# State and offset products of a state-space mixer: fp32 against three fp32r passes in all blocks

## The reference

```python
cb = jnp.einsum('bclgn,bcsgn->bclsg', cc, bc)
y_diag = jnp.einsum('bclsgr,bcsgrp->bclgrp', cb[..., None] * decay, xdt)
decay_to_end = jnp.exp(a_cs[:, :, -1:] - a_cs)
states = jnp.einsum('bclgn,bclgr,bclgrp->bcgrpn', bc, decay_to_end, xdt)
chunk_decay = jnp.exp(a_cs[:, :, -1])
def step(carry, inp):
    st, dec = inp
    return carry * dec[..., None, None] + st, carry
...
y_off = jnp.einsum('bclgn,bcgrpn,bclgr->bclgrp', cc, prev, jnp.exp(a_cs))
```

## Time and profile before

| | us |
|---|---|
| median of 3 runs (lowest, highest) | 2748.22 (2746.03, 2751.57) |
| the profiled execution | 2746.11 |
| its span | 2744.4 |
| PE busy in it | 2702.8 (98%) |
| DVE, ACT, POOL busy | 1587.0, 1228.9, 1098.6 |
| mean granted clock of TensorE | 0.997 |

### The profile page before, as it was taken

The page is one execution under the profiler, slowest core; times in us unless marked ns, Lnnn a source line. Parts: engine busy times, 40 slices in busy tenths (PEclk is TensorE's granted clock), DMA queues, the critical chain, the costliest instruction groups (busy, mean ns, idle before and its releaser), DMA issues.

```text
span 2744.4 us, 37004 instructions
## 1 busy us (share of the span) xinstructions
PE 2702.8 (98%) x13938; PEld 2231.2 (81%) x13938; DVE 1587.0 (58%) x2093; ACT 1228.9 (45%) x2322; POOL 1098.6 (40%) x798
## 2 busy tenths in 40 slices
PE   8999999999999999999999999999999999999998
PEld 6778777888888888888888888888888888888887
DVE  3588742666425665147663466664445666666666
ACT  2366754455424555145542654555445322222323
POOL 1256642133201232003234587765555535353434
PEclk9999999999999999999999999999999999999999
DMA  9687576644556445565436546674434842333323
GB/s 290 200 270 243 202 253 245 264 146 181 201 199 254 179 146 206 193 231 217 167 144 250 187 160 221 240 275 155 164 133 171 345 153 94 142 117 135 118 92 154
DMA packets 225488, 531.10 MB, mean 194 GB/s; under 512 B 14090, under 2 KB 98062, under 8 KB 215838
## 3 DMA queue, kind: packets, MB, share of 16 engines
q1 hardware_dynamic: 225310, 528.74, 53.8%
HBM read 382.74 MB, written 145.95 MB: 193 GB/s over the span
## 4 chain that ended last, share of the span: by engine, by line
PE 92%; ACT 2%; DVE 2%; DMA 1%; issue 1%; SPq 1%; POOL 0%; DVEq 0%; ACTq 0%; POOLq 0%
PE bank L2047 22%; PE bank L2015 22%; PE bank L1725 19%; PE bank L1769 13%; PE bank L1749 6%; PE bank L1840 2%; PE bank L1847 2%; PE bank L1666 1%; PE bank L1821 1%; PE bank L1828 1%; PE bank L1804 1%; ACT E L1418 1%; PE bank L1788 1%; DMA meta_w<-in_w_in 0%; DMA w_scr<-w_both 0%
## 5 line engine op out<-in xcount | busy, mean ns | idle before, releaser
L1725 PE MATMUL bank<-hnT_hi,w_ring 128*128 128x512 f32 x1152 | 374.2, 396 | 0.2 <-DMA w_ring<-w_scr 0.2
L2166 DVE SCALAR_TENSOR_TENSOR acc<-pre,par,acc 128x512 f32<-128x512 f32 x240 | 216.3, 901 | 110.6 <-ACT pre L1276 104.9
L2047 PE MATMUL bank<-w_first,T_hi 128*128 128x512 f32 x896 | 275.9, 389 | 0.0
L1725 PEld LDWEIGHTS bank<-hnT_hi,w_ring 128*128 128x128 f32 x1152 | 216.4, 188 | 45.2 <-ACT win_tmp L1373 0.5
L2015 PE MATMUL bank<-T_hi,w_both 128*128 128x512 f32 x768 | 242.1, 389 | 0.2 <-DVE ff L2427 0.2
L2486 DVE TENSOR_TENSOR acc_th<-bank,acc_th 128x512 f32<-128x512 f32 x224 | 150.0, 686 | 155.3 <-PE bank L2047 155.1
L1769 PE MATMUL bank<-w_ring,T_hi 128*128 128x512 f32 x768 | 239.4, 393 | 0.0
L1029 POOL TENSOR_TENSOR small<-small 128x1 f32<-128x1 f32 (+1 forms) x71 | 17.1, 241 | 534.0 <-ACT yo L1356 334.6
L1725 PE MATMUL bank<-hnT_lo,w_ring 128*128 128x512 f32 x576 | 224.6, 390 | 0.0
L1749 PE MATMUL bank<-w_ring,hnT_hi 128*128 128x384 f32 x768 | 198.2, 339 | 0.0
L527 POOL TENSOR_TENSOR w_both<-raw,w_both 128x1024 fp32r<-128x1024 f32 x52 | 129.4, 2489 | 169.7 <-ACT w_both L519 169.6
(11 more groups left out here) (294 smaller groups left out, 6208.1 us busy)
## 6 DMA issues: line engine op xcount, KB each, us to landing
w_ring<-w_scr SPq DMA_DIRECT2D x312, 512.0 KB, 4.2
T_scr<-stage SPq DMA_DIRECT2D x32, 1792.0 KB, 6.6
w_scr<-w_both SPq DMA_DIRECT2D x104, 512.0 KB, 4.2
pair_raw<-in_w_ff SPq DMA_DIRECT2D x36, 1024.0 KB, 5.4
third<-T_scr SPq DMA_DIRECT2D x28, 1024.0 KB, 4.8
pair_raw<-T_scr SPq DMA_DIRECT2D x28, 1024.0 KB, 4.8
sums<-sums_scr SPq DMA_DIRECT2D x64, 384.0 KB, 4.9
raw<-in_w_in SPq DMA_DIRECT2D x36, 512.0 KB, 6.8
```

Of the source, the lines that this page charges most:

```text
L1725: mm = nc.tensor.matmul(bank[s][:, :], w[:, k, :], t[:, k, :], start=(k == 0 and j == 0), stop=(k == KT - 1 and j == 2))
L2047: mm = nc.tensor.matmul(bank[4 * half + t][:, :], a[:, k, tok], w[:, k, :], start=(SECOND[q % 7] not in GOES_ON and k == 0 and j == 0), st ...
L2166: ins = nc.vector.scalar_tensor_tensor(acc[:, s, 0:TB], pre[:, s, k:k + TB], w, acc[:, s, 0:TB], ALU.mult, ALU.add)
```

## The change

- `y_offset` and the state product become three fp32r passes each, in all four blocks. Their operands get high and low parts in new tiles laid over h: `c_both`, `s_both`, `xw_both`, and two of `b_both` in turn.
- Who makes them, in every step: ACT the high parts of C (128x128), S (128x384) and xw (128x384), and B's high part as a copy of its own (xb shrinks from 512 to 384 columns); POOL the low parts of C and S, ahead of its other mixer work; DVE the low part of B (from PSUM) and of xw.
- PE's step becomes: unit n1, `y_transposes` of q-2, `diagonal` of q-1, `slot1`, `state` of q-1, units n2, `y_offset`. So the fp32 work of a step stands in one stretch. `y_high` and `y_low` move one step later, ahead of xw's parts.
- On ACT the Exp now stands behind the high part of S, which waits for `state_add` of q-1; the high part of xw stands ahead of the block-0 weight splitting and the evacuation of n2. On DVE `state_add` moves ahead of the taps. On POOL S times decay moves ahead of ty += yo.
- The pooling history copies move from DVE to ACT, into the evacuation.
- The load of h moves from item 12 to unit (0, 4) of the out stage, behind the last state product.

```diff
-    def link(self, ins):
+    def mark(self, ins):
         self.n += 1
         ins.then_inc(self.sem, 1)
-        self.eng.wait_ge(self.sem, self.n)
+        return self.n
...
+        s_both = at("s_both", [P, 2, GW], h_at, F32R)
+        xw_both = at("xw_both", [P, 2, GW], h_at + 3072, F32R)
+        c_both = at("c_both", [P, 2, P], h_at + 6144, F32R)
+        b_both = [at(f"b_both{i}", [P, 2, P], h_at + 7168 + 1024 * i, F32R) for i in range(2)]
...
-                        if n == 12:
-
-                            sp.dma_start(h[:, :, :], x_in[0, b * TB:(b + 1) * TB, :].rearrange(
-                                "(t p) d -> p t d", p=P)).then_inc(h_loaded.sem, 16)
...
+                            if (d, i) == (0, 4):
+                                yoff_ps.wait(sp, b, STEPS)
+                                state_ps.wait(sp, b, STEPS)
+                                sp.dma_start(h[:, :, :], x_in[0, b * TB:(b + 1) * TB, :].rearrange(
+                                    "(t p) d -> p t d", p=P)).then_inc(h_loaded.sem, 16)
...
+                        cs_split_hi.wait(pool, b, 2 * q + 1)
+                        nc.gpsimd.tensor_tensor(c_both[:, 1, :], group_tile(g, 1)[:, c * P:(c + 1) * P],
+                                                c_both[:, 0, :].bitcast(F32), ALU.subtract)
+                        cs_split_hi.wait(pool, b, 2 * q + 2)
+                        nc.gpsimd.tensor_tensor(s_both[:, 1, :], S[:, g, :],
+                                                s_both[:, 0, :].bitcast(F32), ALU.subtract
+                                                ).then_inc(s_split_lo.sem, 1)
...
+                        gains_ready.wait(pool, b, 1)
+                        s_split_lo.wait(pool, b, q + 1)
+                        nc.gpsimd.tensor_tensor(by_head(S[:, g, :]), by_head(S[:, g, :]),
+                                                per_head(cd, c, g), ALU.mult
+                                                ).then_inc(scd_ready.sem, 1)
                         if b == 0:
                             low_part(pool, N0 + n2[0] + 2)
                         yo_ready.wait(pool, b, q + 1)
...
+                        yoff_ps.wait(act, b, q)
+                        nc.scalar.activation(c_both[:, 0, :], group_tile(g, 1)[:, c * P:(c + 1) * P],
+                                             ACT.Copy).then_inc(cs_split_hi.sem, 1)
                         sums_loaded[c].wait(act, b, 16 * (g + 1))
...
-                        fall.then_inc(fall_ready.sem, 1)
-                        fall_ready.wait(act, b, q + 1)
+                        falls = steps.mark(fall)
+                        state_ready.wait(act, b, q)
+                        nc.scalar.activation(s_both[:, 0, :], S[:, g, :], ACT.Copy
+                                             ).then_inc(cs_split_hi.sem, 1)
+                        steps.wait(falls)
                         nc.scalar.activation(E[:, :, :], E[:, :, :], ACT.Exp, scale=-1.0
                                              ).then_inc(exp_ready.sem, 1)
 
                         xb_ps.wait(act, b, q + 1)
-                        state_ps.wait(act, b, q)
                         ty_ready.wait(act, b, q)
                         xw_ready.wait(act, b, q)
-                        nc.scalar.activation(xb[:, :], bank[4 + q % 2][:, :], ACT.Copy
+                        nc.scalar.activation(b_both[q % 2][:, 0, :], bank[4 + q % 2][:, GW:GW + P],
+                                             ACT.Copy)
+                        nc.scalar.activation(xb[:, :], bank[4 + q % 2][:, 0:GW], ACT.Copy
                                              ).then_inc(xb_ready.sem, 1)
...
                         if q:
                             y_norm(b, q - 1)
+                        xw_ready.wait(act, b, q + 1)
+                        nc.scalar.activation(xw_both[:, 0, :], xw[:, :], ACT.Copy
+                                             ).then_inc(xw_split_hi.sem, 1)
                         if b == 0:
                             high_part(act, N0 + n2[0] + 2)
...
+                def y_offset(b, q):
+                    s_split_lo.wait(pe, b, q + 1)
+                    for j, (i, o) in enumerate(((0, 0), (0, 1), (1, 0))):
+                        mm = nc.tensor.matmul(bank[7][:, 0:GW], c_both[:, i, :], s_both[:, o, :],
+                                              start=(j == 0), stop=(j == 2))
+                    mm.then_inc(yoff_ps.sem, 1)
...
+                def state(b, q):
+
+                    xw_split_lo.wait(pe, b, q + 1)
                     yo_ready.wait(pe, b, q + 1)
...
                         if n1 is not None:
                             unit(b, n1)
+                        if q > 1:
+                            y_transposes(b, q - 2)
                         if q:
-                            slot3(b, q - 1)
+                            diagonal(b, q - 1)
                         slot1(b, q, g, c)
+                        if q:
+                            state(b, q - 1)
                         for n in n2:
                             unit(b, n)
-                        y_offset(b, q, g, c)
-                        if q:
-                            y_transposes(b, q - 1)
-                    slot3(b, STEPS - 1)
+                        y_offset(b, q)
+                    y_transposes(b, STEPS - 2)
+                    diagonal(b, STEPS - 1)
+                    state(b, STEPS - 1)
...
                         if q:
                             y_finish(b, q - 1)
+                            state_add(b, q - 1)
                         taps(b, n1)
-                        if q:
-                            state_add(b, q - 1)
...
+                        nc.vector.tensor_tensor(b_both[q % 2][:, 1, :], bank[4 + q % 2][:, GW:GW + P],
+                                                b_both[q % 2][:, 0, :].bitcast(F32), ALU.subtract)
...
+                        if q > 1:
+                            y_low(b, q - 2)
+                        xw_low(b, q)
```

More of the change, by code:

```diff
@@ L1246, in _ @@
                 high_part(act, 1)
+                steps = Steps(act, act_sem)
                 def evac(b, v):
@@ L1269, in evac @@
                         w3 = par[:, W_CONV + 60 + ct:W_CONV + 61 + ct]
-                        nc.scalar.activation(pre[:, s, 0:3], hist[:, ct, :], ACT.Copy
-                                             ).then_inc(hist_read.sem, 1)
+                        hist_read = steps.mark(nc.scalar.activation(
+                            pre[:, s, 0:3], hist[:, ct, :], ACT.Copy))
                         nc.scalar.activation(acc[:, s, 0:TB], ps, ACT.Identity, scale=w3,
                                              bias=par[:, W_BIAS + ct:W_BIAS + ct + 1])
-                        hist_read.wait(act, b, sum(conv_tile(m) is not None for m in range(n + 1)))
+                        steps.wait(hist_read)
                         nc.scalar.activation(hist[:, ct, :], ps[:, TB - 3:TB], ACT.Copy)
@@ L1282, in evac @@
                     else:
-                        nc.scalar.activation(pre[:, s, 16:16 + TB], ps, ACT.Copy
+                        i = n - U_POOL
+                        hist_read = steps.mark(nc.scalar.activation(
+                            pre[:, s, 0:16], phist[:, i, :], ACT.Copy))
+                        nc.scalar.activation(pre[:, s, 16:16 + TB], ps, ACT.Copy)
+                        steps.wait(hist_read)
+                        nc.scalar.activation(phist[:, i, :], ps[:, TB - 16:TB], ACT.Copy
                                              ).then_inc(up_evac.sem, 1)
@@ L1817, in slot1 @@
                                      ).then_inc(zc_ps.sem, 1)
-                def y_offset(b, q, g, c):
-                    state_ready.wait(pe, b, q)
-                    nc.tensor.matmul(bank[7][:, 0:GW], group_tile(g, 1)[:, c * P:(c + 1) * P],
-                                     S[:, g, :], start=True, stop=True).then_inc(yoff_ps.sem, 1)
+                def y_offset(b, q):
[4 more added lines that the diff above has]
+                    mm.then_inc(yoff_ps.sem, 1)
                 def y_transposes(b, q):
@@ L1830, in y_transposes, with diagonal @@
                     mm.then_inc(yT_ps.sem, 1)
-                def slot3(b, q):
+                def diagonal(b, q):
                     g_ready.wait(pe, b, q + 1)
@@ L2202, in finish @@
                     up_evac.wait(dve, b, v + 1)
-                    steps.link(nc.vector.tensor_copy(pre[:, s, 0:16], phist[:, i, :]))
-                    steps.link(nc.vector.tensor_copy(phist[:, i, :], pre[:, s, TB:TB + 16]))
                     E_ = TB + 16
```

45 lines of the change are left out of this document (26 added, 19 removed).

## The result

The changed kernel takes 2775.2 us (median of 4 runs, 2774.5 to 2777.5) against 2748.0 for the kernel before (4 runs beside it): a ratio of 1.0099 [1.0085, 1.0113]. It is 27 us slower. The forecast was 2757.5, the range ended at 2774; the rival "the clock joins in" stood at 2774.5. The profiled execution took 2775.5 us with a span of 2773.7, 29.3 more than the span before.

The account below looks back on a forecast made before the run. PE, with 92% of the chain, was taken as the bound, DVE setting block 0's pace after the change. -12.0 - 3.2 + 6 + 14 + 9 - 4.5 = +9.3 gave 2755.4 profiled, 2757.5 as median; range 2725 to 2774.

Parts of the forecast that it names:

- the clock joins in: Rival, chance 0.13: in block 0 y_offset waits over 2 us for S low, lowering the clock; +26.3, so 2774.5 us.
- Products: Blocks 1 to 3: three fp32r passes save PE 0.25 us a step over 48 steps, -12.0 us (-16.3 to -11).
- y one step later: Blocks 1 to 3: a step of slack removes PE's waits of about 0.36 us on y's norm, -3.2 us.
- Last groups of blocks 1 to 3: New waits close a ring there; about 2 us a block stay after slack, +6 us (0 to +10).
- The ring with a pooling tile: Last groups of blocks 1 to 3: in two steps DVE's pooling passes stretch the 8.7 us ring to 9.8 to 10.4.
- h's load: Moving it from item 12 removes PE's 2.8 us wait for S and the slower clock behind: -4.5 us (-4.5 to 0).
- Block 0, first three groups: DVE sets the pace: four steps take 63.1 us against 58.36, so +14 us for three groups (-3 to +24).
- 4.8 us of exclusion in four steps: Block 0, first three groups: POOL's new low parts of S and C, all of which DVE can be made to wait out.
- The order by which the forecast argued: Block 0: Exp waits for state_add, y_finish, ty, POOL's low part, ACT's high part, xw, then Exp again.
- Block 0, last group: Steps stretch from 9.13 us to a ring of 12.3; three intervals and the end, +9 us (+3 to +13).
- The ring of 12.3 us: Block 0, last group: 7.2 us to xw, then xw high 0.45, weight's high part 1.2, low part 2.4, ty += yo 1.0.
- its terms (+24, +13, +9): The clock rival's sizes: block 0's first three groups +24, its last group +13, last groups of the other blocks +9.

Follow-up runs that it names:

- e3: The kernel before with only h's load moved from item 12 into the out stage: 2747.8 us, ratio 1.0000.
- e13: The changed kernel with POOL's S *= cd put back behind ty += yo in block 0: 2756.3 us, ratio 1.0028.
- e11: The changed kernel with PE's transposes of y moved behind the state product of the same step in block 0: 2778.3 us.
- e1: The changed kernel with both products of block 0 in fp32, without their four splits, and S *= cd behind ty += yo there: 2736.9 us.
- e7: The changed kernel with the low parts of C and S in block 0 made by DVE, not POOL: 2783.3 us.
- e15: The changed kernel without DVE's low parts of B and xw in block 0, PE's work kept the same: 2756.4 us.
- e6: The changed kernel with y_offset of block 0 in fp32, no splits of C and S, and S *= cd behind ty += yo there: 2739.9 us.
- e5: The changed kernel with the state product of block 0 in fp32 and no splits of B and xw there: 2757.6 us.
- e17: The changed kernel with block 0's state product in fp32, no splits of B and xw, and S *= cd behind ty += yo there: 2752.3 us.
- e16: The changed kernel with POOL's S *= cd right behind S low in block 0: 2766.7 us, ratio 1.0061.

## Why the prediction was wrong

The sign and the stage were right: blocks 1 to 3 win, block 0 gives back more. In the profiled spans the sum was +9.3 against +29.3 measured. Two steps failed, both on block 0: the size of its first three groups, where DVE's idle time was counted as half free, and a moved product, S *= cd, that was priced at nothing.

- **Products, right.** Plain steps of blocks 1 to 3 are 0.28 to 0.31 us shorter; 0.25 was taken, with 0.23 to 0.34 as its ends.
- **y one step later, right.** The waits of 0.36 on y's norm are gone from all groups but the last. Together with the passes the first three groups of blocks 1 to 3 won 15.8 us, 12.2 were forecast.
- **Last groups of blocks 1 to 3, too small.** The ring with a pooling tile was put at 9.8 to 10.4; from 731.26 to 741.71 (squares of y on ACT) it took 10.45. What slack takes of it was overrated: with the passes' saving these groups cost 2.6, 2.6 and 4.1, 9.2 in all, where +6 less 3.0 for their twelve steps, so +3, was forecast. The three blocks won 6.6, not 9.2.
- **h's load, wrong: 0 for -4.5.** e3 shows why: the wait had successors of nearly its size, and the load costs something in its new place. The lower end of the term was taken; its upper end, 0, was the right one.
- **Block 0, first three groups, the step that failed: +23 for +14.** The two ends for four steps were 57.4 and 66.4 us; measured 66.4. The middle was taken. The upper end had been built as DVE's busy time plus all its idle time, and so it came: 58.4 busy and 8.0 idle. The idle was no slack. It is mostly DVE's wait for ACT's chain (S high, Exp, copies), 10.5 us in eight steps, and ACT waits for DVE's taps in turn. In e13 these four steps had 51.7 busy and 8.3 idle: 6.7 us less of busy time left the idle time as it was.
- **A term that was not there at all.** S *= cd was moved on POOL and got no line in the sum. e13 prices that move at 18.9 us (21.8 in block 0), as much as the whole error of 18 us on the median; with it undone the four steps of group 1 take 59.99 us, under the 63.1 that the forecast took. What was priced, POOL's low parts of C and S as 4.8 us of exclusion in four steps, is smaller, at least for S: without S low block 0 wins 2.1 us in all. C low wasn't taken out by itself. The order by which the forecast argued (the low part behind the high part behind xw behind Exp) is in the trace. What it didn't see is that a delay of about 1 us in it can decide whether DVE or POOL waits out the next 2.4.
- **Block 0, last group: +11 for +9.** The ring of 12.3 us shows as steps of 10.7, 14.1 and 13.5. Its gate was y's low part of the step before, which the forecast didn't name; e11 shows that this made no difference.
- **The clock: right as a rival, not in the forecast.** Waits of 2.1 to 3.7 at `y_offset` came in six steps, and the clock was 0.97, 0.95 and 0.88 in the last three stages, all in all worth about 10 us. It fell at three of these waits (3.7, 3.2 and 2.3 us) and at four of those on y's low part in the last group (4.0, 3.5, 2.9 and 3.3), which the rival didn't name; at the three others at `y_offset` (3.0, 2.4 and 2.1) it stayed at 1.00. The rival's point, waits of about 2 us in most steps with two convolved tiles, was met, and its terms (+24, +13, +9) against +23, +11 and, for the last groups without their saving, +13. Asking what ends DVE's idle time, and whether that waits for DVE, would have moved the chance there.
- **The end: +2.2 not foreseen.** e3, which changes nothing but h's load, waits 1.1 us at the same product behind the last block; e1 doesn't. Its cause is open, and it is about what single runs of one kernel differ by.

What stays open: of which parts the 12.4 us (15.4 by the medians) of the offset's own split are made (S low's absence gives 2.1, and S high's later place 8.1, both measured with S *= cd in its new place), and by how much of e13's gain stems from exclusion and how much from POOL's queue. On exclusion the Trainium skill (SBUF — State Buffer, on the engine ports) says that whichever starts first holds the pair for the whole instruction and the other blocks. The two traces agree, with both outcomes for the same instructions: two finishes and one low part took 3.47 and 2.40 us, or 1.29 and 2.94.

## What to carry to other kernels

Price every instruction that a change moves, also those without new work: ask for each what runs beside it on the engine that it excludes. An engine's idle time is slack only if what ends it doesn't wait for that engine. Where two engines wait for each other in turn, as DVE and ACT do in block 0, new work on the busier one is not hidden: for 13.4 us of DVE's work e7 paid 8 to 10 and e15 got back 19. There the upper bound is the better forecast. In this kernel splitting pays where the other engines have idle time of their own (blocks 1 to 3, 6.6 us) and not where they split weights as well: e1, which leaves block 0 in fp32 and keeps the new order but for S *= cd, takes 2736.9 us against 2748 and 2775.

## What the hardware showed beyond the expectation

- Busy time of DVE fell when it was given more work: 49.2 us in four steps of e6 against 51.8 before, with 3.4 us of new instructions, since fewer of those with two operands in SBUF met POOL's (finishes 6.8 us against 11.2, gate products 7.1 against 9.3).
- The two orders of one meeting differ by 2.2 us on DVE: 1.29 or 3.47 for the same two finishes.
- The place of a product on POOL, S and a row of gains, 1.03 us long, is worth 18.9 us in 16 steps, but 5.3 with the state product in fp32 (medians of e5 and e17); the presence of S low, 1.0 to 1.5 us long, 3 us.
- DVE's product E times cb, with one operand in PSUM, took 0.94 to 0.96 us in every one of the nineteen kernels, also where POOL's S *= cd ran beside it (e16, 222.57 us).
